# Head loop of a two-block model: two low weight parts formed by an adding DMA, query and key quarters exchanged by DMA

## What is computed

```
z = h @ w_in[l]
u_s, q, k, v, g = jnp.split(z, [COL_SSM, COL_Q, COL_K, COL_V], axis=-1)
...
def apply_rope(t, cos, sin):
    t1, t2 = t[..., :half], t[..., half:]
    return jnp.concatenate([t1 * c - t2 * s, t2 * c + t1 * s], axis=-1)
```

## Time and profile before

| | us |
|---|---|
| median of 3 runs | 2191.2 (2190.57 to 2194.05) |
| the profiled execution, its time | 2189.63 |
| its span, first to last instruction | 2187.8 |
| PE busy | 2119.2 (97%) |
| DVE busy | 1150.8 (53%) |
| ACT busy | 997.3 (46%) |
| POOL busy | 794.5 (36%) |

### The profile page before, as it was taken

How to read it: one execution, slowest core, us unless ns; L and a number is a source line. 1 busy time by engine, 2 the same in 40 slices (tenths; PEclk the granted TensorE clock), 3 DMA queues, 4 the chain that set the end, 5 groups by cost and what they waited for, 6 DMA issues and landing times.

```text
span 2187.8 us, 30762 instructions
## 1 busy us (share of the span) xinstructions
PE 2119.2 (97%) x11049; PEld 1737.2 (79%) x11049; DVE 1150.8 (53%) x2127; ACT 997.3 (46%) x1910; POOL 794.5 (36%) x347
## 2 busy tenths in 40 slices
PE   5999999999999999999999999999999999999998
PEld 4788888788888888888888788787777788787876
DVE  5799999474541456442525734232285644232374
ACT  5758787762343442222223434443723434344631
POOL 2511101444464134444443433333334333333342
PEclk9999999999999999999999999999999999999999
DMA  3211212233243122222222222222223222222221
GB/s 143 90 65 53 65 64 63 97 125 97 96 142 109 31 86 77 96 96 96 96 96 101 87 87 78 68 78 72 82 89 128 87 87 78 77 69 77 78 96 58
DMA packets 51731, 189.38 MB, mean 87 GB/s; under 512 B 6564, under 2 KB 7204, under 8 KB 51108
## 3 DMA queue, kind: packets, MB, share of 16 engines
q1 hardware_dynamic: 48096, 175.13, 24.2%
q10 hardware_dynamic: 2452, 6.96, 0.8%
q0 software_dynamic: 1072, 5.77, 0.7%
HBM read 185.74 MB, written 2.10 MB: 86 GB/s over the span
## 4 chain that ended last, share of the span: by engine, by line
PE 80%; DVE 9%; ACT 3%; DVEq 3%; issue 2%; POOL 2%; DMA 1%; ACTq 0%; SPq 0%; POOLq 0%
PE bank L352 22%; PE bank L354 21%; PE bank L353 21%; PE bank L1013 2%; PE bank L1046 2%; PE bank L1027 1%; DVE wide_region L2371 1%; POOL weight_lo L384 1%; ACT wide_region L1132 1%; DVE wide_region L2374 1%; PE bank L421 1%; PE bank L697 1%; PE bank L633 1%; PE bank L651 1%; PE bank L883 1%
## 5 line engine op out<-in xcount | busy, mean ns | idle before, releaser
L384 POOL TENSOR_TENSOR weight_lo<-weight_slots,weight_hi 128x1024 fp32r<-128x1024 f32 x265 | 647.6, 2444 | 965.1 <-ACT weight_hi L378 955.7
L378 ACT ACTIVATE weight_hi<-weight_slots 128x1024 fp32r<-128x1024 f32 x254 | 268.9, 1059 | 794.6 <-PE bank L354 710.4
L352 PE MATMUL bank<-h_hi,weight_hi 128*128 128x512 f32 x1144 | 458.5, 401 | 2.2 <-issue 1.0
L353 PE MATMUL bank<-h_lo,weight_hi 128*128 128x512 f32 x1144 | 446.0, 390 | 0.0
L354 PE MATMUL bank<-h_hi,weight_lo 128*128 128x512 f32 x1136 | 443.0, 390 | 0.0
L352 PEld LDWEIGHTS bank<-h_hi,weight_hi 128*128 128x128 f32 x1144 | 214.7, 188 | 58.0 <-issue 12.7
L354 PEld LDWEIGHTS bank<-h_hi,weight_lo 128*128 128x128 f32 x1136 | 213.3, 188 | 45.6
L353 PEld LDWEIGHTS bank<-h_lo,weight_hi 128*128 128x128 f32 x1144 | 215.1, 188 | 41.5 <-issue 0.5
L384 POOL TENSOR_TENSOR head_weight_lo<-weight_slots,head_weight_hi 128x1024 fp32r<-128x1024 f32 x28 | 67.3, 2407 | 280.2 <-DVE v_region L1826 133.1
L352 PE MATMUL bank<-h_hi,head_weight_hi 128*128 128x512 f32 x336 | 139.0, 414 | 5.8 <-DVE h_lo L401 3.4
L354 PE MATMUL bank<-h_hi,head_weight_lo 128*128 128x512 f32 x336 | 132.0, 393 | 0.0
(11 more groups left out here) (516 smaller groups left out, 4389.8 us busy)
## 6 DMA issues: line engine op xcount, KB each, us to landing
weight_slots<-weights SPq DMA_DIRECT2D x328, 512.0 KB, 3.5
wide_region<-cmp_w ACTq DMA_DIRECT2D x2, 2048.0 KB, 9.1
v_region<-ssm_bc POOLq DMA_DIRECT2D x8, 256.0 KB, 4.0
residual<-x_in POOLq DMA_DIRECT2D x1, 2048.0 KB, 9.3
out<-normed SPq DMA_DIRECT2D x4, 512.0 KB, 2.7
residual<-x_in SPq DMA_DIRECT2D x2, 512.0 KB, 5.3
residual<-x_in ACTq DMA_DIRECT2D x2, 512.0 KB, 9.9
v_region<-mem_in POOLq DMA_DIRECT2D x1, 1024.0 KB, 5.1
```

The lines of the kernel that those rows point to most:

```text
L352: pe.matmul(to, w_h[:, k, :], hi[:, k, 0:width], start=(k == 0), stop=False)
L353: pe.matmul(to, w_h[:, k, :], lo[:, k, 0:width], start=False, stop=False)
L378: act.activation(parts[0][s % 2], slot[s], ACT.Copy).then_inc(w_hi[s], 1)
L384: eng.tensor_tensor(parts[1][at], slot[s], parts[0][at].bitcast(F32), ALU.subtract).then_inc(w_lo[s], 1)
```

## The change

Three things change, all in the head loop, in the bodies of heads 0 to 6 (seven times):

1. The low parts of blocks 3 and 1 are no longer formed on DVE. Right behind the rounded part ACT runs `weight_negated`: it goes over the slot once more, with scale -1 and a float32r result, into the low part's buffer; POOL issues a DMA that adds the slot onto it (`weight_add`), and after its landing POOL raises `w_lo[s]` (`weight_added`).
2. ACT's four quarter copies per query and key are gone (head 0's own, ahead of the loop, stay). POOL waits for the plain tile and issues four DMAs of 32 x 512 from it into the exchanged tile (`swap_quarters`).
3. DVE's `rope` waits for these four landings instead of for `evac_done`.

```diff
+        def weight_negated(act, s, parts):
+            act.activation(parts[1][s % 2], slot[s], ACT.Copy, scale=-1.0).then_inc(w_neg, 1)
+        def weight_add(pool, n, s, parts):
+            pool.wait_ge(w_neg, n)
+            pool.sem_inc(w_neg_seen, 1)
+            pool.dma_start(parts[1][s % 2], slot[s], accum_op=ALU.add).then_inc(w_lo_added, 16)
+        def weight_added(pool, n, s):
+            pool.wait_ge(w_lo_added, 16 * n)
+            pool.sem_inc(w_lo[s], 1)
...
-            def head_evac(hd, s):
+            def head_evac(hd, s, negated=False, swaps=False):
                 if s < 3:
                     ahead(act, hd + Q_HEAD, s, W_HEADS)
+                if negated:
+                    weight_negated(act, 3, W_HEADS)
...
-                    for quarter in range(4):
+                    for quarter in range(4) if swaps else ():
...
-            def head_values(hd, dst=VT_H):
+            def head_values(hd, dst=VT_H, negated=False):
                 ...
                 ahead(act, hd + Q_HEAD, 3, W_HEADS)
+                if negated:
+                    weight_negated(act, 1, W_HEADS)
...
-                    head_evac(b + 1, 1)
+                    head_evac(b + 1, 1, True)
...
-                    head_values(b + 1)
+                    head_values(b + 1, negated=True)
...
             def rope(hd, i):
-                dve.wait_ge(evac_done[i], hd + (Q_HEAD + 1))
+                dve.wait_ge(rope_swapped[i], 64 * hd)
...
                 s5_scan(b)
-                if not last:
-                    weight_lo(dve, b + (Q_HEAD + 1), 3, W_HEADS)
                 row_max(2)
...
                 da_combine(b, 3)
-                if not last:
-                    weight_lo(dve, b + (Q_HEAD + 2), 1, W_HEADS)
...
+            def swap_quarters(hd, i):
+                raw, swapped = ((QRAW, QSW), (KRAW, KSW))[i]
+                pool.wait_ge(evac_done[i], hd + (Q_HEAD + 1))
+                pool.sem_inc(raw_seen, 1)
+                for quarter in range(4):
+                    other = quarter ^ 1
+                    pool.dma_start(swapped[32 * quarter:32 * quarter + 32, :],
+                                   raw[32 * other:32 * other + 32, :]).then_inc(rope_swapped[i], 16)
...
                 weight_lo(pool, b + (Q_HEAD + 1), 2, W_HEADS)
+                swap_quarters(b + 1, 0)
                 next_input(b + 1)
+                weight_add(pool, 2 * b + 1, 3, W_HEADS)
+                swap_quarters(b + 1, 1)
+                weight_added(pool, 2 * b + 1, 3)
                 pool.wait_ge(gen_ready, b + 2)
                 weight_lo(pool, b + (Q_HEAD + 2), 0, W_HEADS)
+                weight_add(pool, 2 * b + 2, 1, W_HEADS)
+                weight_added(pool, 2 * b + 2, 1)
```

More of the change, by code:

```diff
@@ L281, in build @@
         rope1_in = sem("rope1_in")
+        w_neg, w_neg_seen, w_lo_added = sem("w_neg"), sem("w_neg_seen"), sem("w_lo_added")
+        rope_swapped, raw_seen = sems("rope_swapped", 2), sem("raw_seen")
         x_again, out_ready = sem("x_again"), sem("out_ready")
@@ L1172, in _ @@
                     head_values(0, PR[0])
-                head_evac(0, s)
+                head_evac(0, s, swaps=True)
             act.drain()
```

## The result

The changed kernel takes 2208.04 us (median of 4 runs, 2207.63 to 2208.81) against 2190.89 (2190.2 to 2194.05): ratio 1.0079, 95% interval 1.0067 to 1.0091, 17.1 us slower. The forecast was 2206. The profiled execution has a span of 2206.0 us, 18.2 more than before.

What follows compares the result with a forecast made beforehand. PE, 97% busy, bounds it, waiting in the heads only for DVE's run to L1937. The late query exchange costs 7 x 2.26 = 15.8 us: 2189.6 + 15.8 = 2205.4, named 2206; eight in ten within 2192 to 2221.

Steps and rivals of the forecast that it cites:

- DVE's run from the maxima to L1937 decides: In each head, gapless DVE work from 230.25 to 246.59 sets when PE starts L697, 0.50 us late.
- The pitch of POOL's issues, 0.96: POOL's four query DMAs start 0.96 us apart, lower bound 0.56, so the fourth issue begins at 236.4.
- 64 KB land in 3.0: Query's fourth DMA lands 3.0 us after issue, bounds 2.5 and 4.9, completing the exchange at 239.4.
- The split into a fixed part and a part by size, 2.5: Landing estimate: 2.3 us independent of size plus 1.4 per 512 KB, so 64 KB would take 2.5.
- the predicted 15.8: Loss before the s5 output products: L697 starts 2.26 us later in each of seven heads, 15.8 us.
- The clock: Rival, chance 0.04: PE's 2.7 us idle per head drops the clock to 1.2 GHz, adding 2 to 4 us per head.
- The row I argued from the earlier trace: Evidence against a clock fall: a stretch with 1.5 of 8 us idle kept the full 2.4 GHz.
- Key and adding DMAs are covered; the adding DMA lands like 1024 KB, 5.1: Key's exchange has 2 to 3 us cover before DVE asks; adding DMAs, priced at 5.1 us, land before PE needs them.
- Block 3 is worth PE's 3.8 us, block 1 nothing: Removing DVE's block 3 low part, 1.14 us, gains PE's 3.8 us wait over seven heads; block 1's gains nothing.
- Signs named beforehand: Heads 39 to 41 us, L697 waits 2 to 4, DVE idle 2 to 5 before query's rotation, issues 0.9 to 1.0 apart.
- ACT's relief is worth nothing: ACT has net 2.7 us less work per head, but PE waits for it nowhere, so no gain.
- The sum of 10 us: Alternative loss using the Trainium skill's 2.15 us for 64 KB: query's exchange lands at 238.55, 10 us in all.

Runs made afterwards that it cites:

- the last two runs: Query on ACT's copies, key by DMA, against the version with both adding DMAs: adding DMA for block 3 only, 2187.71 us; for block 1 only, 2191.63 us.
- the second experiment: Changed kernel with the query's and key's exchanges back on ACT's copies, only the two adding DMAs kept: 2191.25 us, ratio 1.0002.
- the run with block 1 alone: Query on ACT's copies, key by DMA, adding DMA for block 1 only, block 3's low part back on DVE: 2191.63 us, ratio 1.0002.

## Why the prediction was right

The way and the mechanism were right, the one given as the likeliest. That the number is within 2 us is luck: two of its terms were mis-sized, their sum was 4 us short, and a rival that had been given 0.04 was true as well and filled the gap.

- *DVE's run from the maxima to L1937 decides, and the query's exchange stands in it.* Right: 2187.95 when the query alone goes back.
- *The pitch of POOL's issues, 0.96.* Wrong: 0.51. The one pair in the earlier trace rows carried 0.40 us of something else.
- *64 KB land in 3.0.* Too short for this place: 3.8 from the fourth issue. The split into a fixed part and a part by size, 2.5, was not too low; alone the quarters take 1.9. What the prediction had wrong is the company. It let the fourth DMA leave "after most of the slot's reload has passed"; with issues 0.51 apart it leaves at 242.49, 1.3 behind the start of that load (241.19).
- The two errors hang together and have opposite signs (1.35 too much, 0.8 too little). DVE was to stand 3.4 us and stood 2.8, L1937 was to be 2.26 late and PE's waits grew by 12.1 / 7 = 1.7. The sum of the waits was 4 us below the predicted 15.8.
- *The clock*, 0.04, priced at 2 to 4 us per head: it fell in five of seven heads, at 1.2 us each. Those 6 us filled the gap. The row I argued from the earlier trace rows had 1.5 us of idle time within 8; one piece of 2.0 to 2.3 us was already enough in most heads, though one of 2.95 and one of 2.0 passed without a fall.
- *Key and adding DMAs are covered; the adding DMA lands like 1024 KB, 5.1.* Right: 5.0, no wait at the key.
- *Block 3 is worth PE's 3.8 us, block 1 nothing.* Right, by the last two runs (3.4 us and nothing), and by where PE's wait is.
- *Signs named beforehand.* Heads of 39 to 41 us, PE's waits of 2 to 4, DVE's idle of 2 to 5 all held; the issues 0.9 to 1.0 apart did not. DVE is busy 2.1 us less per head (2.4 named), ACT 3.3 less (2.7 named).
- *ACT's relief is worth nothing.* Right for the change as a whole, but the reason was too broad: ACT is not so free that it could carry the negated copies without being rid of the key's, as the second experiment shows.
- The Trainium skill, "DMA: Bandwidth & Descriptors", anatomy of one SWDGE DMA: its fit gives 2.15 us for 64 KB. POOL's queue took 1.8 to 2.2 (median 1.9) where nothing shared the DMA engines, which is near it, and 3.8 from the fourth issue in the changed kernel, where the slot's load ran beside it. The sum of 10 us that the prediction worked out from it was for this second case.

## What to carry to other kernels

Taking work off a busy engine helps only up to the next engine's slack (here 0.5 us a head), while a transfer put in the work's place costs its whole chain: the wait for the issuing engine, the issues one after another, and the landing, which for 64 KB was 1.9 us alone and 3.8 beside a 512 KB load. Look at what starts that load: here it was the end of the very low part that the exchange had to wait for, so being late and being slow came together. Before moving an operation in a shared stretch, look at what the neighbours run beside it: the low part on POOL stood exactly beside the four DVE operations that it doesn't block, and starting it 0.6 us later cost 22 us over the seven heads, more than the thing to be gained. And where PE would stand in one piece, as here for 2.0 to 2.3 us, count the clock on top of the wait.

## What was not expected of the hardware

- DVE's two-input operation on SBUF tiles is held by one of POOL's: 2.81 and 2.89 us in place of 0.68, with the start of POOL's operation 0.15 and 0.16 us before it.
- The landing of 64 KB from SBUF to SBUF hangs on what runs beside it and hardly on the queue: 1.9 us from POOL's queue and 2.0 from ACT's with the DMA engines free, 3.8 from POOL's beside a load of 512 KB. In the run with block 1 alone, one head has both: the key's first three quarters, issued from 240.86 on, land in 1.8 to 1.9 us, the fourth, issued 0.2 us ahead of a slot's load, in 2.7.
- The clock falls after single waits of PE of 2.0 to 2.3 us in most heads, and filling the wait with idle products gives 4 us back. The rest of the program varies too: the versions with the query on ACT's copies and on ACT's queue reach the last s5 output products at 392.76 and 392.79 us, where the kernel before has 397.02, yet their profiled spans are 2187.3 and 2183.3. Of the 4.3 us won in the heads, the first of these executions has lost 3.8 behind them, where PE is busy 3.3 us longer than in the second with the same products; that this is the clock fits, but was not tested. The gain of 3 us is therefore that of the medians of eleven runs.
